# Attention scores of two heads at a time, and the mask added by VectorE in the instruction that takes the maximum

## What is computed

```python
# first block, 12 heads a layer ("att1" in the kernel)
s = where(key <= query, q @ k.T * scale, -1e30);  p = softmax(s)
# second block, "diff": 8 maps a layer
s = where(chunk(key) <= chunk(query), q @ k.T * scale, -inf);  p = softmax(s)
# second block, "fox": 8 heads a layer
s = q @ k.T * scale + cum_log_f[query] - cum_log_f[key]
p = softmax(where(key <= query, s, -inf))
```

## Time and profile before

| | us |
|---|---|
| median of 3 runs (1227.13 to 1230.93) | 1230.49 |
| the profiled execution | 1235.84 |
| its span, first to last instruction | 1234.0 |
| PE busy | 1191.6 |
| DVE busy | 747.2 |
| ACT busy | 628.7 |
| POOL busy | 111.0 |

### The profile page before, as it was taken

How to read it: one execution, slowest core, us unless ns; L and a number is a source line. 1 busy time by engine, 2 the same in 40 slices (tenths; PEclk the granted TensorE clock), 3 DMA queues, 4 the chain that set the end, 5 groups by cost and what they waited for, 6 DMA issues and landing times.

```text
span 1234.0 us, 17788 instructions
## 1 busy us (share of the span) xinstructions
PE 1191.6 (97%) x7018; PEld 1021.1 (83%) x7018; DVE 747.2 (61%) x1161; ACT 628.7 (51%) x989; POOL 111.0 (9%) x98
## 2 busy tenths in 40 slices
PE   8899989999999999989999999999999899999997
PEld 5788779889887798779998988888977678889776
DVE  4886657655557867576555565567544655675445
ACT  5434555544545434745454445646545446465462
POOL 0323010000001322100000000003000000030000
PEclk9989899999999979999999999999999999999999
DMA  8524235566555424236666555534433435444321
GB/s 283 169 67 158 98 103 171 178 196 186 180 187 178 127 86 137 86 106 219 188 187 187 188 154 171 185 108 136 136 104 103 137 120 182 126 131 126 108 97 69
DMA packets 88763, 180.72 MB, mean 146 GB/s; under 512 B 8664, under 2 KB 19800, under 8 KB 88680
## 3 DMA queue, kind: packets, MB, share of 16 engines
q1 hardware_dynamic: 87240, 175.32, 45.7%
q10 hardware_dynamic: 1440, 4.26, 1.0%
HBM read 178.51 MB, written 1.05 MB: 146 GB/s over the span
## 4 chain that ended last, share of the span: by engine, by line
PE 79%; DVE 12%; issue 3%; ACT 3%; POOL 1%; DMA 1%; POOLq 0%; DVEq 0%; SPq 0%; ACTq 0%
PE bank L745 21%; PE bank L747 21%; PE bank L746 21%; PE bank L861 3%; PE bank L822 2%; DVE w_lo L1538 2%; PE bank L970 1%; PE bank L873 1%; DVE vecs L1547 1%; ACT w_hi L1172 1%; PE bank L866 1%; DVE xn L1816 1%; PE bank L864 1%; PE bank L1098 1%; PE bank L881 1%
## 5 line engine op out<-in xcount | busy, mean ns | idle before, releaser
L1538 DVE TENSOR_TENSOR w_lo<-raw,w_hi 128x1024 fp32r<-128x1024 f32 x296 | 366.2, 1241 | 302.0 <-ACT w_hi L1172 298.5
L1172 ACT ACTIVATE w_hi<-raw 128x1024 fp32r<-128x1024 f32 (+1 forms) x320 | 335.2, 1052 | 247.3 <-PE bank L747 211.8
L745 PE MATMUL bank<-h_hi,w_hi 128*128 128x256 f32 x896 | 262.6, 293 | 1.7 <-DVE w_lo L1538 1.7
L746 PE MATMUL bank<-h_lo,w_hi 128*128 128x256 f32 x896 | 257.6, 288 | 0.0
L747 PE MATMUL bank<-h_hi,w_lo 128*128 128x256 f32 x896 | 257.4, 287 | 0.0
L745 PE MATMUL bank<-w_hi,h_hi 128*128 128x512 f32 (+1 forms) x448 | 182.0, 406 | 5.4 <-DVE h_lo L1557 5.4
L745 PEld LDWEIGHTS bank<-h_hi,w_hi 128*128 128x128 f32 x896 | 176.6, 197 | 3.5 <-DVE w_lo L1538 2.3
L746 PEld LDWEIGHTS bank<-h_lo,w_hi 128*128 128x128 f32 x896 | 176.3, 197 | 0.5
L747 PEld LDWEIGHTS bank<-h_hi,w_lo 128*128 128x128 f32 x896 | 176.0, 196 | 0.0
L747 PE MATMUL bank<-w_hi,h_lo 128*128 128x512 f32 (+1 forms) x448 | 175.2, 391 | 0.0
L746 PE MATMUL bank<-w_lo,h_hi 128*128 128x512 f32 (+1 forms) x448 | 174.6, 390 | 0.0
(11 more groups left out here) (296 smaller groups left out, 1655.2 us busy)
## 6 DMA issues: line engine op xcount, KB each, us to landing
raw<-in_w_in SPq DMA_DIRECT2D x144, 512.0 KB, 3.9
raw<-in_w_ff SPq DMA_DIRECT2D x128, 512.0 KB, 4.1
raw<-in_w_out SPq DMA_DIRECT2D x40, 512.0 KB, 3.3
raw<-in_cmp_w SPq DMA_DIRECT2D x8, 512.0 KB, 4.4
raw<-in_w_in SPq DMA_DIRECT2D x8, 404.0 KB, 4.2
x_sb<-in_x SPq DMA_DIRECT2D x2, 512.0 KB, 7.4
gain<-in_norm_ffn ACTq DMA_DIRECT2D x2, 512.0 KB, 6.4
gain<-in_pre_norm ACTq DMA_DIRECT2D x2, 512.0 KB, 5.6
```

The lines of the kernel that those rows point to most:

```text
L745: pe.matmul(out_ap, s_hi, m_hi, start=start, stop=False, **kw)
L746: pe.matmul(out_ap, s_hi, m_lo, start=False, stop=False, **kw)
L1172: act.activation(slot(w_hi, u), slot(raw, u), ACT.Copy).then_inc(hi_ready, 1)
L1538: dve.tensor_tensor(slot(w_lo, u), slot(raw, u), slot(w_hi, u).bitcast(F32), ALU.subtract)\
```

## The change

- Heads 2n and 2n+1 share one S: `score_pair` (a new function of PE's program) opens both banks and issues for each query block first the even head's product, then the odd head's, so that consecutive products use different row groups. Their E is at one place too, that of the even head; T and V stay where they were.
- PE no longer adds a mask. DVE's `row_max` runs one instruction for each query block that reads the scores from PSUM and a mask from SBUF (`C_FREE`, zeros, lies ahead of `C_CAUSAL` so that one pattern reads zeros and then the mask), writes the sum into `probs` and yields its maximum. The built program has a second DVE instruction behind each, which reads the maximum out. `row_max` frees the bank.
- ACT's exponentials work in place on `probs`; T waits for `exp_ready`.
- fox's two bias products a block become one: `row_stack` holds the rounded rows and the rests in partitions 0 to 39 and again in 64 to 103, and the selector is laid out alike, so the bias of a head uses 40 rows of its own row group. `m_rows` becomes one product a head likewise. For this the selector's DMA grows from 8 to 104 rows (32 KB to 416 KB), the constants' by 64 KB, fox's DVE preparation by one copy and one subtraction, and POOL clears `row_stack` once.
- Two of the four bf16 casts go. The warm-up on PE is 44 matmuls of 256 columns in place of 22 of 512.

```diff
+LOWEST = -3.0e38
+STACK = 104
-C_ID, C_CAUSAL, C_CHUNK, C_STRICT, C_LE, C_RTRI, C_ONES, C_NONES = (128 * n for n in range(8))
+C_ID, C_FREE, C_CAUSAL, C_CHUNK, C_STRICT, C_LE, C_RTRI, C_ONES, C_NONES = (128 * n for n in range(9))
...
-        if stage == "S":
-            use((*name, "S", h), 4 + h % 2)
+        if stage == "S" and h % 2 == 0:
+            for c in range(2):
+                use((*name, "S", h + c), 4 + c)
...
-                    if start[h] + lag == p:
+                    first = start[h - h % 2] if stage in ("E", "S") else start[h]
+                    if first + lag == p:
...
+            def score_pair(kind, l, h):
+                pair = [((kind, l, "S", h + c), *heads_of(kind, l)[h + c]) for c in range(2)]
+                ps = [open_bank(key) for key, *_ in pair]
+                last = "bias" if kind == "fox" else "scores"
+                blocks = ((0, 0), (P, 1))
+                for lo, i in blocks:
+                    cols = (i + 1) * P
+                    for c, (key, q, k, *_) in enumerate(pair):
+                        mm = pe.matmul(ps[c][:, lo:lo + cols], q[:, i * P:(i + 1) * P], k[:, 0:cols], start=i == 0,
+                                       stop=i == 1 and last == "scores", skip_group_check=True)
...
+                if last == "bias":
+                    for lo, i in blocks:
+                        cols = (i + 1) * P
+                        for c in range(2):
+                            r = slice(64 * c, 64 * c + 40)
+                            mm = pe.matmul(ps[c][:, lo:lo + cols], sel[r, (h + c) * P:(h + c + 1) * P], row_stack[r, 0:cols],
+                                           start=False, stop=i == 1, skip_group_check=True)
...
-                    link(act.activation(probs[:, h % 3, 0:P], ps[:, 0:P], ACT.Exp, scale=SCALE,
+                    link(act.activation(slot_p[:, 0:P], slot_p[:, 0:P], ACT.Exp, scale=SCALE,
...
-                link(dve.tensor_reduce(row_mx[:, h % 2, 0:1], ps[:, 0:P], AX.X, ALU.max))
-                link(dve.tensor_reduce(row_mx[:, h % 2, 1:2], ps[:, P:3 * P], AX.X, ALU.max))
+                link(dve.tensor_tensor_reduce(dst[:, 0:P], ps[:, 0:P], const[:, mask:mask + P], 1.0, LOWEST, ALU.add, ALU.max,
+                                              mx[:, 0:1]))
+                seen_ = const[:, C_FREE:C_FREE + 2 * (mask - C_FREE)].rearrange("p (b c) -> p b c", b=2)[:, :, 0:P]
+                free(dve.tensor_tensor_reduce(dst[:, P:3 * P].rearrange("p (b c) -> p b c", b=2),
+                                              ps[:, P:3 * P].rearrange("p (b c) -> p b c", b=2), seen_, 1.0, LOWEST,
+                                              ALU.add, ALU.max, mx[:, 1:2]), key)
...
-                        for n, c in enumerate((C_ID, C_CAUSAL, C_CHUNK, C_STRICT)):
+                        for n, c in enumerate((C_ID, C_STRICT)):
```

More of the change, by code:

```diff
@@ L52 @@
 SLOTS = 4
-WARM = 22
+WARM = 44
+LOWEST = -3.0e38
+STACK = 104
 SECOND_LOADS = 6
@@ L388, in side2 @@
                     for h in range(8):
-                        if int(first + sp * h) + lag == p:
+                        lead = h - h % 2 if stage in ("E", "S") else h
+                        if int(first + sp * lead) + lag == p:
                             head_steps(name, h, stage, groups_of)
@@ L571, in hybrid_blocks @@
         ident = const[:, C_ID:C_ID + P]
-        ident_b, causal_b, chunk_b, strict_b = (masks[:, n * P:(n + 1) * P] for n in range(4))
+        ident_b, strict_b = (masks[:, n * P:(n + 1) * P] for n in range(2))
         def conv_col(l, tap, c):
@@ L900, in _ @@
             for n in range(WARM):
-                pe.matmul(bank[6][:, :], masks[:, 0:P], masks[:, :], start=True, stop=True)
+                pe.matmul(bank[6][:, 0:2 * P], masks[:, 0:P], masks[:, :], start=True, stop=True)
             pe.wait_ge(ident_loaded, 16)
@@ L2010, in _ @@
                         if s[2] == "S":
-                            row_max((kind, l), s[3])
+                            row_max((kind, l), s[3], C_CHUNK if kind == "diff" else C_CAUSAL)
                         elif s[2] == "V" and s[3] % GROUPS[kind] == GROUPS[kind] - 1:
```

99 lines of the change are left out of this document (53 added, 46 removed).

## The result

The changed kernel takes 1176.85 us (median of 4 runs, 1173.15 to 1181.94) against 1230.71 of the kernel before beside it; the ratio is 0.9568, 95% interval [0.954, 0.9596]. That is 53.9 us less, where 35.6 were predicted, and the range of 1182 to 1212 misses it on the fast side. The profiled execution of after took 1181.94 us with a span of 1180.1, so the two profiled spans also differ by 53.9.

A forecast was written before the change was run, and what follows sets the result against it. PE was taken as the bound in the second block, with DVE also near its limit in att1. Savings of 10.4 + 19.7 + 6.0 - 0.5 = 35.6 us from 1230.49 gave 1195 us, range 1182 to 1212.

The forecast's parts named there:

- Scores of diff: Second block, diff heads: a pair takes 1.20 us instead of 2.50; eight pairs in two layers save 10.4 us (3.2 to 11.6).
- Full overlap, 1.45: Upper bound for a diff pair: both heads' 1.05 us score streams run fully side by side, saving 1.45 us.
- The trailing of 0.15: In a pair, the second head's stream starts 0.15 us late, 0.074 for each of two matmuls ahead of it.
- Scores of fox: Second block, fox heads: a pair takes 1.60 us instead of 4.06 with fewer bias matmuls; eight pairs save 19.7 us.
- What hides the rest: Second block: two projection units between S and T hide DVE's and ACT's work for both heads; priced at nothing.
- att1, 6.0: att1: PE saves 15.6 us over twelve pairs, but DVE's limits and waits leave 3.0 a layer, 6.0 in all.
- The wait of 2.87: att1: PE's 2.87 us wait at 143.25 for an exponential behind the SiLU goes, as that exponential now stands ahead.
- The start: Kernel start: DMAs grow by 448 KB while two mask casts go; a loss of 0.5 us (0 to 1.6).
- Strict order: Rival, chance 0.12: matmuls start in program order even across row groups, so a pair takes 1.35 us; 1198.5 us.
- No overlap: Rival, chance 0.12: the two heads' streams don't run side by side, only masks and rest rows go; 1216.5 us.
- DVE as the bound: Rival, chance 0.04: DVE limits att1; from 1.23 us more a head the kernel is slower, at 1.5 it takes 1237.
- att1 is PE's as well: Rival, chance 0.06: DVE's new instructions cost no more than the old, all 15.6 us in att1 count; 1185 us.

The follow-up runs named there:

- more filler: Changed kernel plus bf16 products with unused results, ahead of att1's 15-column cmp products and at nine of PE's waits: 1169.16 us, ratio 0.9496.

## Why the prediction was wrong, point by point

The direction, the overlap and the hidden work were right; every price of a score product was taken from a row with masks in it, and att1 was discounted by guesses that were too high. Of the 18 us missed, 5 to 7 are the pair's price in the second block and the rest att1, where the same price and the clock have a share too.

- **Scores of diff, 10.4: right in kind, too small.** 8 x 1.64 = 13.1. The step that failed is "1.05 of them scores": a stream takes 0.85, and 0.20 of the 1.05 was the masks' effect on their neighbours, read as score time because only distances between starts were at hand. "Full overlap, 1.45" was no bound for the same reason.
- **The trailing of 0.15: wrong.** It came from two stages of other products and was read as a price for each product ahead; the second stream starts 0.007 behind in alternating order and 0.013 in the other. The first of those stages has products of 128 rows (128*128 in its line), both halves of the array and no single row group, so the two were not alike; and the second stream there began 0.47 after the first, not 0.59.
- **Scores of fox, 19.7: too small.** 8 x 2.97 = 23.8: the same stream and trailing, and the bias pair of 0.23 where 0.40 was taken from rows of 8-row products.
- **What hides the rest: right.** 14 us of DVE more cost nothing. Only the wait of 0.71 us a layer at a T of fox wasn't foreseen. Second block in all: 37.3, less 1.8 lost ahead of it and between its layers, 30.1 predicted.
- **att1, 6.0: wrong, and most of the miss.** The stretches gain 18.1, 12.1 more. Three things make that up: the product count was too small as in diff (12 x 1.30 = 15.6; by the same rows 20.2), 4.6; the stretches stood at 1.2 GHz for less time in the one profile than in the other, some 3, which differs from run to run by more than that and is luck; and 9.6 were deducted where PE's idle time grew by 5.4, 4.2. DVE's 0.28 a head was 0.01, and DVE's busy time in the four stretches even fell from 191.2 to 185.8. The wait ahead of the cmp stage was to rise by 2.6 to some 4 and comes to 1.93 in three parts, 0.9 more. The 1.1 us that DVE was to be late in 106 to 136.8 are 2.2, at the cmp keys. The wait of 2.87 was to go and is 2.2 in two parts; in the second layer it was 1.2 and is 2.2 as well. The order that was to end it changes 0.2 of it. So single deductions were wrong in both directions.
- **The start, -0.5: 0.2 gained.** The wait of 1.64 at 37.48 is gone in after, where PE comes there later by a longer stretch at 1.2 GHz (5.7 us where before had 3.0); with the full clock (more filler) the same 1.64 us stand there again. The run with masks behind the pair, which makes four casts, has them at the clock of after too. So the casts and the clock both seem to count; no run settles which.
- **The rivals.** Strict order is out by its own run. No overlap would have cost 13.0. DVE as the bound: half or more of what is added in att1 counts, but nothing near 1.23 us a head was added. "att1 is PE's as well" was the nearest, with 1185.

## What to carry to other kernels

Price a product from a row in which it stands alone, and not from the distance to the next one where that has other rows or another type: a small product of 128 rows between two of 64 cost four times its columns here, and behind both no more than they. Two streams of 64 rows in different row groups cost as much as one. Where an engine beside the one that is made faster sets the pace, as in att1, a large part of the same saving turns into waits, and here the clock stayed up once the waits were filled; filler at a place where PE waits anyway is worth a try there.

## What the runs showed of the hardware that was not expected

- Two fp32 streams of 64 rows in different row groups take 0.86 us together and 0.85 one alone; alternating in one row group they take 1.51.
- A 128-row bf16 product of 128 columns costs 0.05 us behind 64-row fp32 products and 0.20 between them.
- DVE's sum with maximum takes as long as the maximum alone (424 and 425 ns), with a read-out of 83 ns that overlaps its end; a head's maxima take DVE 0.87 us as against 0.86.
- A change from 64 rows to 128 between f32 products costs some 0.09 us; from bf16 to f32 at 128 rows none is seen (0.03 from start to start).
- A stream in a second row group started ahead of three records of the first that stand before it in the program, in two traces.
- A bf16 product of 256 columns between 15-column fp32 products costs 0.03 us, and 64 of them made a kernel 5 us faster, since PE stayed at 2.4 GHz for longer (granted clock 0.986 against 0.981).
